# A ninth 2 MB slot for the expert weights, loaded ahead of the expert stage

## Chip, cores and metric

One core of one Trainium2 chip runs the whole program. The metric is device time in microseconds (us), the median of several runs. Engines are named as the profile names them: PE (TensorE matmul), PEld (its weight load), DVE (VectorE), ACT (ScalarE), POOL (GpSimd), SP (SyncE, which here only issues DMAs).

## What is computed

The reference runs two blocks on 256 tokens of width 1024, all in float32.

The first block has two layers of a mixer (attention, a spatial gate, a Fourier mix) and a squared-ReLU MLP, over the tokens and over 256 context tokens.

The second block projects the tokens (`w_in_2`), runs a gated linear recurrence and a chunked linear attention, sums both through `w_out_2`, and normalises. Then comes the mixture of experts:

```python
logits = xt @ w_router + b_router
top_val, top_idx = lax.top_k(logits, TOP_K)          # 4 of 32 experts for each token
...
hdn = xb @ w_up[e] + b_up[e]                         # 1024 -> 2048
gate_h = jnp.minimum(hdn[:, :D_FF_2], SWIGLU_LIMIT)
up_h = jnp.clip(hdn[:, D_FF_2:], -SWIGLU_LIMIT, SWIGLU_LIMIT)
act = (up_h + 1.0) * gate_h * jax.nn.sigmoid(SWIGLU_ALPHA * gate_h)
y = act @ w_down[e] + b_down[e]                      # 1024 -> 1024
```

A second layer norm and a gate through `w_ple_gate` end it. The weights of one expert are 8 MB (`w_up`) and 4 MB (`w_down`); all 32 experts are read, whatever the router chooses.

## The kernel before

Every weight matrix is cut on the host into chunks of 2 MB, 128 partitions by 4096 floats (`CW = 4096`). A chunk lies in a slot of SBUF, and PE reads it from there. `ring(s)` (line 159) says where slot s lies: slots 0 to 2 are the tile RG, slots 3 to 6 are the four quarters of the tile BIG, slot 7 is the end of SM1, and slot 8 is another piece of BIG, used once in the first block. Up to the end of the second block's mixer only the three slots of RG turn over, because BIG holds intermediate results. For the experts eight slots are used: 3, 4, 5, 6, the three of RG in the order in which they come free, then 7. `R.turn` (line 1125) is that order, and chunk i of the expert stage lies in slot `R.turn[i % 8]`. Expert e has the chunks 6e to 6e+5: four of `w_up`, then two of `w_down`. After the 192 chunks of the experts come the two of `w_ple_gate`, numbers 192 and 193. They must lie in slots 3 and 4, since other data lies in the rest of BIG by then.

All weight loads are issued by one engine, SP, in one order (from line 2887). It first walks through the list of early chunks, waiting before each one until PE has finished with the chunk that was in its slot. The last two early chunks are those of `w_out_2`. Then it waits for `s_ym` (line 2915), which DVE raises eight times as it finishes the mixer's output; from there on BIG is free. It loads two small constants, then chunks 0 to 3 into BIG. Chunks 4 to 6 wait for the three RG slots; chunk 7 waits until SM1's end is free (`("z", 7)`, `("pw", 7)`), with the small load of `b_up_rows` between the two waits. From chunk 8 on, chunk i waits for `s_used` to reach i - 7. PE raises `s_used` by one when it has finished a chunk, so load i starts when PE is done with chunk i - 8:

```python
                if i >= 8:
                    sp.wait_ge(s_used, i - 7)
                landing(key, source(key))
```

`landing` (line 2887) starts the DMA, which raises `s_landed` of its slot by 16 when it has landed; `expert_chunk` (line 1127) has PE wait for that before the first matmul on the chunk.

In the expert stage PE does for each expert (`expert`, line 1244): a bias matmul, the scatter of the expert before, 8 matmuls of 128x512 on each of the four `w_up` chunks (line 1275; the profile has 16 records for them), the transposes and the gather for the next expert (lines 1162, 1138, 1297), and 8 matmuls on each of the two `w_down` chunks (line 1312). Expert 1 has more than 64 tokens in this input and takes a wider path (lines 1183 to 1239). DVE and ACT do the activation (lines 2632, 1921, 1929). POOL does nothing in this stage. ACT issued three DMAs (lines 1803 to 1805) earlier; POOL issues none.

Of the kernel before, what the change touches and what calls it, by code (L numbers as in the profile page):

```python
# [12 lines left out]
NEXP = 32  # L13
CW = 4096
# [78 lines left out]
class Ring:  # L93


    def __init__(self):
        self.order, self.slot, self.nth, self.count, self.end, self.now, self.before = [], {}, {}, [0] * 9, {}, {}, {}

    def get(self, key, slot):
        if key not in self.slot:  # L100
# [17 lines left out]
def build(nc, A, out):  # L118
    (T1, W1), (T2, W2) = smalls()
    ctx = ExitStack()  # L120
    with ctx:
        def sb(name, w, p=128):
            return ctx.enter_context(nc.sbuf_tensor(name, [p, w], F32))

        def sem(name):
            return ctx.enter_context(nc.semaphore("s_" + name))
# [4 lines left out]
        CAT_ = sb("CAT", 4096)  # L131
        BIG = sb("BIG", 16384)
        RG = sb("RG", 3 * CW)
        STAT = sb("STAT", 512 * 3)
        MISC = sb("MISC", 1100)
        HOLD = sb("HOLD", 1024)
# [19 lines left out]
        def s2(n, *dims):  # L156
            o, w = T2[n]
            return view(SM1, o, *(dims or (w,)))

        def ring(s):  # L160
            if s < 3:
                return RG[:, s * CW:(s + 1) * CW]
            if s < 7:
                return BIG[:, (s - 3) * CW:(s - 2) * CW]
            if s == 8:
                return BIG[:, 7680:7680 + CW]
            return SM1[:, W2 - CW:W2]

        def own(t, s):
# [3 lines left out]
        s_full = [sem(f"full{i}") for i in range(8)]  # L173
        s_free = [sem(f"free{i}") for i in range(8)]

        s_landed = [sem(f"landed{i}") for i in range(9)]
        s_used = sem("used")
        s_cc, s_sm, s_sm2, s_sm3, s_out = (sem(n) for n in ("cc", "sm", "sm2", "sm3", "out"))

# [66 lines left out]
        F, R = Fills(range(8)), Ring()  # L246
# [36 lines left out]
        WS2 = [view(SM1, o + 512 * i, 4, 128) for i in range(2)]  # L283
        WS4 = [view(STAT, 256 + 768 * i, 4, 128) for i in range(2)]
        AS1, AS2, AS4 = (view(CAT_, 1024 * i, 4, 256) for i in range(3))
# [48 lines left out]
        def stat(s, slot):  # L334
            return STAT[:, 768 * s + 256 * slot:768 * s + 256 * slot + 256]

# [48 lines left out]
        c4b = SV[:, 400:408].rearrange("p (a e) -> p a e", a=2)  # L385
        GTT = STAT[:, 1024:1280]
        IOTA, IOTA2, TRI, ONE1 = HOLD[:, 256:384], HOLD[:, 384:512], HOLD[:, 768:896], onet[:, 0:128]
# [17 lines left out]
        SELG2 = SM1[:, 768:1024].rearrange("p (a s) -> p a s", a=2)  # L405
        SCT = STAT[:, 1280:1536]
        G1_, S1_ = (view(STAT, 512 * i, 2, 256) for i in range(2))
        U1_ = view(HOLD, 0, 2, 512)[:, :, 0:256]
# [31 lines left out]
        def _(pe):  # L440
# [681 lines left out]
            hints = {}  # L1122
            over = pe.alloc_register("pe_over")
            ended = list(F.at)
            R.turn = [3, 4, 5, 6] + sorted(range(3), key=lambda s: ended.index(R.end[R.now[s]])) + [7]

            def expert_chunk(ex, c):
                i = 6 * ex + c
                s, nth = R.get(("expert", ex, c), R.turn[i % 8])
                pe.wait_ge(s_landed[s], 16 * nth)  # L1130
                return ring(s).rearrange("p (k n) -> p k n", k=4)

# [267 lines left out]
                m = pe.matmul(banks[b][:, 0:256], ones, XS[:, k, 0:256], start=k == 0, stop=k == 7)  # L1400
            m.then_inc(s_zfull[b], 1)
            for c in range(2):
                s, nth = R.get(("w_ple_gate", c), R.turn[(6 * NEXP + c) % 8])
                assert s in (3, 4)
                pe.wait_ge(s_landed[s], 16 * nth)
                w = ring(s).rearrange("p (k n) -> p k n", k=8)
                for n in range(4):
                    b = end_take(("e", 4 * c + n))
                    for k in range(8):
                        if c + n == 0:  # L1410
                            pe.wait_ge(s_zg, k + 2)
                        pe.matmul(banks[b][:, 0:257], w[:, k, 128 * n:128 * n + 128], ZG[:, k, :], start=k == 0, stop=False)  # L1412
                    pe.matmul(banks[b][:, 256:257], ID2, s2("b_ple")[:, 4 * c + n:4 * c + n + 1],
                              start=False, stop=True).then_inc(s_zfull[b], 1)
                    if c == 0 and n == 1:
                        b = end_take(("ms",))
                        pe.wait_ge(s_zsum, 7)
                        pe.matmul(banks[b][:, 0:256], ones, SIDE[:, 0, :], start=True, stop=True).then_inc(s_zfull[b], 1)
# [585 lines left out]
        def _(dve):  # L2004
# [354 lines left out]
            post("ff", 0, X)  # L2359
            D.up(dve.memset(STAT[:, 256:257], 1.0))  # L2360
            one = D.n
# [523 lines left out]
        @block.sync  # L2885
        def _(sp):
            def landing(key, src):
                sp.dma_start(ring(R.slot[key]), src).then_inc(s_landed[R.slot[key]], 16)

            def full(key):  # L2890
                b, n, m = F.at[key]
                sp.wait_ge(s_full[b], m)

            def source(key):
                if key[0] == "expert":
                    return A["w_up"][key[1], key[2]] if key[2] < 4 else A["w_down"][key[1], key[2] - 4]
                if len(key) == 2:
                    return A[key[0]][key[1]]
                if key[0].startswith("w_ff"):
                    return A[f"{key[0]}_{key[1]}"][key[2]]  # L2900
                return A[f"{key[0]}{key[1]}"][key[-1]]

            first = T1["ropec"][0]
            sp.dma_start(SM1[:, 0:first], A["sm1"][:, 0:first]).then_inc(s_cc, 16)
            sp.dma_start(own(XS, C), A["xs"][:, C]).then_inc(s_in[C], 16)
            early = [k for k in R.order if k in R.end]
            for i, key in enumerate(early):
                if R.before[key]:
                    full(R.end[R.before[key]])
                landing(key, source(key))  # L2910
                if key == ("w_in", 0, C, 0):
                    sp.dma_start(own(XS, X), A["xs"][:, X]).then_inc(s_in[X], 16)
                if key == ("w_in", 0, C, 1):
                    sp.dma_start(SM1[:, first:W1], A["sm1"][:, first:W1]).then_inc(s_sm, 16)
            sp.wait_ge(s_ym, 8)
            sp.dma_start(HOLD[:, 256:512], A["iota"]).then_inc(s_sm3, 16)
            sp.dma_start(HOLD[:, 768:896], A["tri"]).then_inc(s_sm3, 16)
            for i in range(6 * NEXP + 2):
                key = ("expert", i // 6, i % 6) if i < 6 * NEXP else ("w_ple_gate", i - 6 * NEXP)
                if 4 <= i < 7:  # L2920
                    full(R.end[R.now[R.turn[i]]])
                if i == 7:
                    full(("z", 7))
                    sp.dma_start(BUPR, A["b_up_rows"]).then_inc(s_sm3, 16)
                    full(("pw", 7))
                if i >= 8:
                    sp.wait_ge(s_used, i - 7)
                landing(key, source(key))
            for k0, k1 in (0, 4), (4, 7), (7, 8):
                sp.wait_ge(s_fin, k1)  # L2930
                sp.dma_start(out[:, k0:k1, :], ZO[:, k0:k1, :]).then_inc(s_out, 16)
            sp.wait_ge(s_out, 48)
# [137 lines left out]
```

## Time and profile before

| what | value |
|---|---|
| time, median of 3 runs | 2335.0 us (2332.87 to 2336.21) |
| the profiled execution's own time | 2330.96 us |
| its span, first to last instruction | 2329.2 us |
| granted TensorE clock, mean | 0.996 |
| PE busy | 2224.1 us (95% of the span) |
| DVE, ACT, POOL busy | 771.6, 463.3, 154.1 us |
| read from HBM | 598.20 MB |

The profile is of one execution. Times within it count from the first instruction of the span. The share of DMA is the mean busy share of the core's 16 DMA engines. An idle time stands with what ended it: "<-DMA RG<-in_w_up" says that the engine went on when a load of `w_up` into RG had landed. The chain of waits is followed back from the last instruction, at each step to what released it. In the chain a DMA piece runs from its issue to its landing, so it holds the time in the queue too.

### The profile page before, as it was taken

What the parts mean: (1) busy time and instruction counts of PE and PEld (TensorE: products, weight loads), DVE (VectorE), ACT (ScalarE), POOL (GpSimd) and SP (SyncE); (2) the same over time, 40 slices, a digit from 0 to 9 for tenths busy, and PEclk for the clock granted to TensorE, in tenths of its full rate; (3) what the DMA queues carried; (4) which work ended last, traced back from release to release, by engine and by line L of the source; (5) the groups of instructions that cost most, each with busy time, mean ns of one, the idle gap of its engine ahead of it and who ended that gap; (6) DMA issues with size and microseconds to landing.
All of it is one profiled execution on the core that took longest, in us unless ns stands there. A gap on an engine that the chain in (4) does not pass through costs nothing.

```text
span 2329.2 us, 27569 instructions
## 1 busy us (share of the span) xinstructions
PE 2224.1 (95%) x11292; PEld 1450.0 (62%) x11292; DVE 771.6 (33%) x1789; ACT 463.3 (20%) x1056; POOL 154.1 (7%) x162
## 2 busy tenths in 40 slices
PE   6999999999999999999999999999999899999998
PEld 4777888888887688887688843334333333333335
DVE  2245554578525420004665321112111111111114
ACT  3255411100024532002543210000000000000003
POOL 1000111144301000000000000000000000000000
PEclk9999999999999999999999999999999999999999
DMA  9722212134215444434433768999999999999993
GB/s 387 272 107 109 109 73 109 73 117 173 109 73 193 178 177 165 156 145 175 144 109 143 292 272 343 427 427 427 427 428 427 427 428 428 425 429 428 427 428 141
DMA packets 44264, 601.16 MB, mean 258 GB/s; under 512 B 4705, under 2 KB 7521, under 8 KB 7905
## 3 DMA queue, kind: packets, MB, share of 16 engines
q1 hardware_dynamic: 43696, 595.40, 63.0%
q10 hardware_dynamic: 432, 3.87, 0.4%
q8 instruction: 95, 1.56, 0.3%
q14 instruction: 41, 0.33, 0.0%
HBM read 598.20 MB, written 1.05 MB: 257 GB/s over the span
## 4 chain that ended last, share of the span: by engine, by line
PE 78%; DMA 18%; DVE 2%; ACT 1%; issue 0%; POOL 0%; SPq 0%; POOLq 0%; PEldq 0%; DVEq 0%; ACTq 0%
PE PS L1275 11%; DMA RG<-in_w_up 9%; PE PS L961 8%; DMA BIG<-in_w_up 8%; PE PS L706 7%; PE PS L1312 6%; PE PS L741 6%; PE PS L690 5%; PE PS L793 5%; PE PS L654 3%; PE PS L539 3%; PE PS L779 2%; PE PS L1138 2%; PE PS L1171 2%; PE PS L478 1%; PE PS L1412 1%
## 5 line engine op out<-in xcount | busy, mean ns | idle before, releaser
L2632 DVE TENSOR_SCALAR STAT<-PS 128x256 f32<-128x256 f32 x64 | 27.2, 424 | 709.1 <-PE PS L1275 688.6
L1275 PE MATMUL PS<-BIG,XS 128*64 128x512 f32 x1024 | 230.2, 599 | 23.6 <-DMA BIG<-in_w_up 23.6
L1275 PE MATMUL PS<-RG,XS 128*64 128x512 f32 x768 | 172.6, 597 | 20.2 <-DMA RG<-in_w_up 20.2
L1275 PEld LDWEIGHTS PS<-BIG,XS 128*64 128x64 f32 x1024 | 70.4, 137 | 173.1 <-issue 125.9
L961 PE MATMUL PS<-XS,RG 128*128 128x256 f32 x768 | 173.2, 384 | 5.0 <-DVE XS L2075 4.1
L1461 ACT ACTIVATE BIG<-PS 128x256 f32<-128x256 f32 (+2 forms) x197 | 82.2, 432 | 442.1 <-PE PS L706 138.9
L961 PEld LDWEIGHTS PS<-XS,RG 128*128 128x128 f32 x768 | 146.6, 193 | 26.8 <-issue 6.9
L1921 ACT ACTIVATE STAT<-STAT 128x256 f32<-128x256 f32 x64 | 26.6, 416 | 592.8 <-DVE STAT L2632 592.8
L2041 DVE TENSOR_SCALAR HOLD<-PS 128x256 f32<-128x256 f32 x27 | 11.4, 423 | 380.0 <-PE PS L514 277.9
L1275 PEld LDWEIGHTS PS<-RG,XS 128*64 128x64 f32 x768 | 52.1, 136 | 131.7 <-issue 92.2
L690 PE MATMUL PS<-HN,RG 128*128 128x256 f32 x576 | 125.1, 379 | 1.0 <-ACT HN L1510 1.0
L690 PEld LDWEIGHTS PS<-HN,RG 128*128 128x128 f32 x576 | 109.3, 190 | 16.5 <-issue 1.7
L1312 PE MATMUL PS<-BIG,CAT 128*64 128x512 f32 x512 | 115.1, 598 | 0.8 <-DVE CAT L2658 0.8
L793 PE MATMUL PS<-BIG,RG 128*128 128x256 f32 x512 | 110.7, 379 | 0.0
L793 PEld LDWEIGHTS PS<-BIG,RG 128*128 128x128 f32 x512 | 97.3, 190 | 13.2
L2793 POOL TENSOR_TENSOR HN<-HN 128x256 f32<-128x256 f32 x84 | 63.2, 752 | 629.8 <-ACT HN L1489 206.4
L1312 PE MATMUL PS<-RG,CAT 128*64 128x512 f32 x384 | 86.5, 597 | 0.0
L1312 PEld LDWEIGHTS PS<-BIG,CAT 128*64 128x64 f32 x512 | 34.3, 136 | 69.8 <-issue 60.0
L706 PE MATMUL PS<-HN,RG 128*128 128x256 f32 x336 | 77.3, 379 | 0.0
L539 PE MATMUL PS<-HN,RG 128*128 128x256 f32 x320 | 73.0, 382 | 0.0
L654 PE MATMUL PS<-CAT,RG 128*128 128x256 f32 x320 | 71.5, 381 | 0.0
L706 PEld LDWEIGHTS PS<-HN,RG 128*128 128x128 f32 x336 | 63.8, 190 | 8.7
(400 smaller groups left out, 3251.2 us busy)
## 6 DMA issues: line engine op xcount, KB each, us to landing
BIG<-in_w_up SPq DMA_DIRECT2D x64, 2048.0 KB, 34.1
RG<-in_w_up SPq DMA_DIRECT2D x48, 2048.0 KB, 33.8
BIG<-in_w_down SPq DMA_DIRECT2D x32, 2048.0 KB, 35.4
RG<-in_w_ff SPq DMA_DIRECT2D x31, 2048.0 KB, 7.8
RG<-in_w_ada SPq DMA_DIRECT2D x24, 2048.0 KB, 8.7
RG<-in_w_down SPq DMA_DIRECT2D x24, 2048.0 KB, 35.4
RG<-in_w_in SPq DMA_DIRECT2D x23, 2048.0 KB, 7.9
SM<-in_w_up SPq DMA_DIRECT2D x16, 2048.0 KB, 35.2
```

The source lines that it names most:

```text
L539: m = pe.matmul(banks[b][:, 0:256], w[:, k, c0:c0 + 128], N[:, k, :], start=k == 0, stop=k == 7)
L654: m = pe.matmul(banks[b][:, 0:256], w[:, k, 128 * (n % 4):128 * (n % 4) + 128], own(CAT, s)[:, k, :], start=i == 0, stop=i == 7)
L690: m = pe.matmul(banks[b][:, 0:256], w[:, k, 128 * n:128 * n + 128], own(HN, s)[:, k, :], start=k == 0, stop=k == 7)
L706: m = pe.matmul(banks[b][:, 0:256], w[:, k, :], a[:, k, :], start=not first and k == 0, stop=k == 3, skip_group_check=True)
L741: return pe.matmul(banks[b[j]][:, 256 * half:256 * half + 256], w, a, start=first and half == 0, stop=last, skip_group_check=True)
L779: m = pe.matmul(banks[b[s, o]][:, 0:256], w[:, k, 128 * o:128 * o + 128], own(FFH, s)[:, 16 * h + k, :], start=h + k == 0, stop=h * 16 + k ...
L793: m = pe.matmul(banks[b][:, 0:256], w[:, k, :], own(FFH, s)[:, k, :], start=k == 0, stop=k == 31)
L961: m = pe.matmul(banks[b][:, 0:256], w[:, k, 128 * n:128 * n + 128], src[:, k, 0:256], start=k == 0, stop=k == 7)
L1275: i = pe.matmul(banks[b][64 * h:64 * h + 64, :], XG[:, 4 * (c % 2) + kk, 64 * r:64 * r + 64], w[:, kk, 512 * h:512 * h + 512], start=False ...
L1312: m = pe.matmul(banks[b][64 * h:64 * h + 64, :], AVT[:, i:i + 64], w[:, kk, 512 * h:512 * h + 512], start=c + kk == 0, stop=c == 1 and kk ...
L1461: i = act.activation(dst, banks[b][rows, part], fn)
L2793: S.up(pool.tensor_tensor(H[:, i, :], H[:, i, :], H[:, k, :], ALU.add))
```

## The change

The bookkeeping `Ring` has counters for ten slots. A new tile EXT of 4096 floats (16 KB per partition, 2 MB in all) is allocated behind RG and becomes slot 9. There is one more landing semaphore. The program reserves 1,024 bytes per partition for the descriptors of DMAs that POOL would issue, in place of the default of 16,384.

The expert stage uses nine slots in the order 9, 5, 6, 3, 4, the three of RG, 7. SP issues chunk 0 into slot 9 behind the last early chunk, ahead of its wait for `s_ym`. Chunks 1 to 4 follow the small constants, chunks 5 to 7 wait for RG, chunk 8 for SM1's end, and from chunk 9 on load i waits until PE is done with chunk i - 9. Chunks 192 and 193 fall on slots 3 and 4 as before. The amount of data is the same.

```diff
+        EXT = sb("EXT", CW)
...
+            if s == 9:
+                return EXT[:, :]
...
-        s_landed = [sem(f"landed{i}") for i in range(9)]
+        s_landed = [sem(f"landed{i}") for i in range(10)]
...
-            R.turn = [3, 4, 5, 6] + sorted(range(3), key=lambda s: ended.index(R.end[R.now[s]])) + [7]
+            R.turn = [9, 5, 6, 3, 4] + sorted(range(3), key=lambda s: ended.index(R.end[R.now[s]])) + [7]
...
-                s, nth = R.get(("expert", ex, c), R.turn[i % 8])
+                s, nth = R.get(("expert", ex, c), R.turn[i % 9])
...
+            landing(("expert", 0, 0), source(("expert", 0, 0)))
             sp.wait_ge(s_ym, 8)
             sp.dma_start(HOLD[:, 256:512], A["iota"]).then_inc(s_sm3, 16)
             sp.dma_start(HOLD[:, 768:896], A["tri"]).then_inc(s_sm3, 16)
-            for i in range(6 * NEXP + 2):
+            for i in range(1, 6 * NEXP + 2):
                 key = ("expert", i // 6, i % 6) if i < 6 * NEXP else ("w_ple_gate", i - 6 * NEXP)
-                if 4 <= i < 7:
+                if 5 <= i < 8:
                     full(R.end[R.now[R.turn[i]]])
-                if i == 7:
+                if i == 8:
                     full(("z", 7))
                     sp.dma_start(BUPR, A["b_up_rows"]).then_inc(s_sm3, 16)
                     full(("pw", 7))
-                if i >= 8:
-                    sp.wait_ge(s_used, i - 7)
+                if i >= 9:
+                    sp.wait_ge(s_used, i - 8)
                 landing(key, source(key))
...
-    nc = bacc.Bacc("TRN2", target_bir_lowering=False, num_devices=1)
+    nc = bacc.Bacc("TRN2", target_bir_lowering=False, num_devices=1, dynamic_dma_scratch_size=1024)
```

## Rows read from the trace of the kernel before

**Rows 1.** The page's head: busy time of each engine over the span.

```profile
PE 2224.1 (95%) x11292; PEld 1450.0 (62%) x11292; DVE 771.6 (33%) x1789; ACT 463.3 (20%) x1056; POOL 154.1 (7%) x162
```

**Rows 2.** Busy time by stretches: start:end, length, engines, PEclk, DMA share, GB/s.

```profile
1275.00:1297.00 22.00, 22.00 (x110) 19.52 (x109) 12.96 (x26) 5.29 (x11) 0.00 (x0) 1.00 0.26 96
1340.00:1356.00 16.00, 15.27 (x103) 10.40 (x103) 4.55 (x23) 4.93 (x10) 0.00 (x0) 0.93 0.02 7
1356.00:1431.00 75.00, 71.38 (x526) 30.01 (x528) 14.61 (x40) 6.35 (x11) 0.00 (x0) 1.00 0.86 337
1431.00:1645.00 214.00, 214.00 (x1084) 83.93 (x1082) 40.80 (x112) 16.23 (x32) 0.00 (x0) 1.00 1.00 425
1645.00:2290.00 645.00, 589.49 (x2911) 221.02 (x2908) 112.56 (x308) 44.02 (x87) 0.00 (x0) 1.00 1.00 426
```

**Rows 3.** PE's waits from 1645 to 2290 us: us in total, times, longest.

```profile
PE PS L1275 <- DMA BIG<-in_w_up: 23.6, 19, 2.8
PE PS L1275 <- DMA RG<-in_w_up: 20.2, 18, 1.2
PE PS L1275 <- DMA SM<-in_w_up: 8.6, 7, 1.2
```

**Rows 4.** The chain of waits in the expert stage: start, length, what.

```profile
1352.34 3.58 PE PS L1275 x16
...
1585.86 13.88 PE PS L1275 x64
...
1612.34 13.88 PE PS L1275 x64
...
1645.88 35.20 DMA RG<-in_w_up
...
1763.31 35.24 DMA RG<-in_w_up
...
1822.05 36.80 DMA BIG<-in_w_up
...
2236.30 35.26 DMA RG<-in_w_up
```

**Rows 5.** PE's timeline, first waits: start, length, [idle before <- what ended it].

```profile
1638.76 7.09 PE L1275 MATMUL PS<-RG,XS 128*64 128x512 f32 x32
...
1676.24 3.65 PE L1275 MATMUL PS<-RG,XS 128*64 128x512 f32 x16 [1.07 <-DMA RG<-in_w_up]
1681.13 3.65 PE L1275 MATMUL PS<-RG,XS 128*64 128x512 f32 x16 [1.24 <-DMA RG<-in_w_up]
```

**Rows 6.** PE's timeline at the end of the last expert.

```profile
2271.60 3.65 PE L1275 MATMUL PS<-RG,XS 128*64 128x512 f32 x16 [1.24 <-DMA RG<-in_w_up]
...
2281.38 3.65 PE L1312 MATMUL PS<-SM,CAT 128*64 128x512 f32 x16
...
2293.43 3.71 PE L1412 MATMUL PS<-BIG 128*128 128x257 f32 x16 [1.21 <-ACT BIG L1974]
```

**Rows 7.** SP's DMA issues from 1255 us on: start, from first to last issue.

```profile
1257.25 17.94 SPq L2888 DMA_DIRECT2D RG<-in_w_out  x2
1297.41 0.33 SPq L2916 DMA_DIRECT2D HOLD<-in_iota  x1
...
1298.26 2.08 SPq L2888 DMA_DIRECT2D BIG<-in_w_up  x4
...
1333.46 0.33 SPq L2888 DMA_DIRECT2D SM<-in_w_up  x1
1355.97 5.84 SPq L2888 DMA_DIRECT2D BIG<-in_w_up  x2
```

**Rows 8.** DMA queues (packets, MB, share); one source's loads, KB each, us to landing.

```profile
q1 hardware_dynamic: 43696, 595.40, 63.0%
q10 hardware_dynamic: 432, 3.87, 0.4%
...
RG<-in_w_out SPq DMA_DIRECT2D x8, 2048.0 KB, 7.9
```

More of the change, by code:

```diff
@@ L96, in __init__ @@
     def __init__(self):
-        self.order, self.slot, self.nth, self.count, self.end, self.now, self.before = [], {}, {}, [0] * 9, {}, {}, {}
+        self.order, self.slot, self.nth, self.count, self.end, self.now, self.before = [], {}, {}, [0] * 10, {}, {}, {}
     def get(self, key, slot):
@@ L1402, in _ @@
             for c in range(2):
-                s, nth = R.get(("w_ple_gate", c), R.turn[(6 * NEXP + c) % 8])
+                s, nth = R.get(("w_ple_gate", c), R.turn[(6 * NEXP + c) % 9])
                 assert s in (3, 4)
```

## The prediction

> **What bounds the kernel now.** I read the page's head first. PE is busy for 95% of the span [rows 1], which suggests that only PE work counts. The stretches say otherwise for the last 650 us [rows 2]. From 1431 us on the DMA engines have a share of 1.00 and bring 425 or 426 GB/s, up to 2290 us. In the first part of that, up to 1645 us, PE is busy without a gap. In the second it is idle for 645.00 - 589.49 = 55.5 us. PE's own waits name the cause of 52.4 us of it (23.6 + 20.2 + 8.6): loads of w_up that had not landed [rows 3]. There are 44 such waits, two per expert.
>
> The chain of waits gives the two speeds [rows 4]. Before 1645 us it runs through PE alone, and one expert takes 1612.34 - 1585.86 = 26.48 us. After 1645 us each piece of about 35 us is a DMA, from issue to landing. Two experts then take 1822.05 - 1763.31 = 58.74 us, which is 12 chunks, so one chunk takes 4.895 us of the DMA queue and one expert 29.37 us. DMA is slower than PE by 2.89 us per expert. PE starts with eight chunks in hand, lives on them until 1645.9 us, and from there runs at the speed of the queue. The last wait of this kind ends at 2271.60 us [rows 6]. What follows is fixed work behind the last loads.
>
> So the end is set by a full queue: the moment from which it never runs empty, plus the chunks that it still has to bring, at 4.895 us each. The change must be priced by what it does to this sum. PE's busy share says nothing on it.
>
> **Where the queue is not full.** Chunks 0 to 3 are issued at 1298.26 us, and the issue for chunk 7 is at 1333.46 us [rows 7]. From 1340 to 1356 us the DMA share is 0.02 [rows 2]: all eight slots are full, and PE has not finished a chunk. At 1355.97 us it has, and chunk 8 is issued. From 1356 to 1431 us the share is 0.86: a load starts whenever PE ends a chunk, and the queue sometimes runs dry. From 1431 us on it never does. Ahead of all this, from 1275 to 1297 us, the share is 0.26 and the rate 96 GB/s: that is the second chunk of w_out_2, issued at 1257.25 + 17.94 - 0.33 = 1274.86 us, and then nothing. SP stands at its wait for s_ym there.
>
> **The change, part by part.**
>
> 1. Chunk 0 moves ahead of the wait for s_ym. SP issues it at about 1275.2 us, just behind the second chunk of w_out_2. That chunk lands 7.9 us after its issue by the median [rows 8], at 1282.8 us, and chunk 0 one transfer later, at about 1287.7 us. The queue was empty then and stays empty until 1297.41 us, so the 4.9 us of transfer cost nothing. The issue takes 0.33 us of SP, which waits there for some 22 us. It holds back nothing: s_ym releases SP at 1297.4 us as before.
>
> 2. The loads behind the wait keep their times and shift by one in number. At 1298.26 us four loads into BIG go out, now chunks 1 to 4. The three RG slots get chunks 5 to 7 as they come free, as they got 4 to 6. Then b_up_rows goes out with as many bytes ahead of it as before, and SM1's end gets chunk 8 at 1333.46 us. When PE ends its first chunk at 1355.97 us [rows 7], chunk 9 is issued where chunk 8 was. PE is not held up by loads before 1645.9 us, so it ends every chunk at the old time up to there, and every issue up to there stands where it stood. The queue sees the same transfers at the same times up to 1431 us and is full afterwards. Chunk i + 1 therefore lands when chunk i landed before. From the last chunk's view: **-4.9 us**.
>
> 3. Bounds of this term. The transfer of one chunk in a full queue is 4.895 us [rows 4]. The most that one chunk can be worth is its time from an empty queue, 7.9 us [rows 8], if its start-up were saved as well. The least is 0, if the lead is lost somewhere before the queue is full. I take the full-queue value, since chunks 9 and on stand in a full queue.
>
> 4. One more DMA wait is postponed. With a chunk more in hand, PE reaches the queue's speed later. Without its waits PE would come to the chunk that it waited for at 1676.24 us [rows 5] at 1638.76 + 7.09 + 26.48 = 1672.3 us. That chunk now lands at 1676.2 - 4.9 = 1671.3 us, in time. The next one lands at 1681.1 - 4.9 = 1676.2 us, and PE comes for it at about 1675.9 us. So the first wait moves from 1646 to about 1676 us, and the waits of rows 3 fall by 4.9, from 52.4 to about 47.5 us. This is the same 4.9 us seen from PE, not a second gain.
>
> 5. The order 9, 5, 6, 3, 4 in place of 3, 4, 5, 6, one more semaphore, and the counters: 0. Chunks 1 to 4 wait for the same event and all of BIG comes free with it; landing semaphores cost PE one wait per chunk as before. Should the order matter after all, there is room: PE starts on chunk 0 at 1352.34 us [rows 4], and chunk 4 should land some 22 us after its issue at 1298.26 us (7.9 + 3 x 4.9).
>
> 6. The smaller reserve for descriptors: 0. It serves DMAs that POOL issues; the queues are those of SP and ACT [rows 8], and POOL issues none. EXT moves other tiles to other addresses, which no row prices; I take 0.
>
> 7. The end. The last expert's third and fourth w_up chunks, its w_down chunks and those of w_ple_gate all land 4.9 us earlier. PE runs from 2271.60 us by its own work except for the last w_down chunk, whose matmuls start at 2281.38, just two transfers after 2271.60, so that one moves with the queue as well. The gate's matmuls at 2293.43 us wait for ACT [rows 6], which moves with PE.
>
> Sum: -4.9 us. Against the profiled execution's own time, 2330.96 us, that gives 2326.1 us, and a span of 2324.3. The median of the runs is 4.0 us above the profiled execution, so I predict **2330.1 us**.
>
> **A rule weighed against a row.** For HBM to SBUF transfers the Trainium skill, "SBUF — State Buffer", section "Summary: rules for kernel authors", says to reckon with about 358 GB/s. By that figure a chunk of 2,097,152 bytes would take 5.86 us, an estimate from that page, and the sum would be -5.9 us. The trace disagrees: 425 to 426 GB/s stand over the whole full stretch [rows 2], and 4.895 us per chunk in the chain. The measured value is used.
>
> **The rivals.**
>
> A. No gain: 2335.0 us. The lead would be lost before 1431 us, for instance because PE's releases come later, or because the profile's empty stretch is not empty in other runs. For it: the stretch from 1356 to 1431 us is bound by releases and not by bytes. Against it: an empty stretch that keeps its place costs the new kernel what it cost the old one. Chance 0.06.
>
> B. The bubbles mean too few buffers, and with one more the queue is better used. Each of the 44 waits would go, and the time would be 2335.0 - 52.4 = 2282.6 us. Against it: the DMA share is 1.00 during these very waits [rows 2, 3], so there is no idle time of the queue to fill. Chance 0.01. The Trainium skill, "Perfetto Trace Analysis", section "Identifying the Most-Contended Engine", reads repeating bubbles on the engine that should be busy as a possible sign of too little SBUF for the next tile; by that rule this rival is the natural reading, and the trace speaks against it.
>
> C. More than one chunk, by some 3 to 6 us: the start-up of a load in the release-bound stretch is saved as well, -7.9 us or somewhat more, 2327 us or less. For it: the share of 0.86 there. Against it: issues and depth of the queue are the same there. Chance 0.04.
>
> D. Slower. One DMA piece of the chain took 36.80 us in place of 35.24 [rows 4], so now and then a chunk needs 1.56 us more. Of the pieces between 1645.88 and 2236.30 us two of eleven are of this kind. Up to eight loads are in flight in the full stretch now; there will be nine. If the longer queue brought such a hiccup once in nine chunks, from about 1676 us on, then (2271.6 - 1676) / 4.9 = 121 chunks would have 13.5 of them, 21 us, and the sum would be 21 - 4.9 = +16 us: 2351 us. It decides from the fourth extra hiccup on (4.9 / 1.56 = 3.1). Nothing in the rows ties the hiccups to depth: between 1645 and 2236 us the depth is the same everywhere, and they are rare. Chance 0.03.
>
> **How the numbers follow.** The forecast case has 0.86. A measurement of this kernel can tell about 0.2% from no change, which is 4.7 us; the forecast of 4.9 us lies just beyond that bound. The three runs of before spread over 3.3 us, so a median may be off by one or two. Of the 0.86 I give 0.47 to faster by over 0.2% and 0.39 to within 0.2%. A adds 0.06 to the same, B and C 0.05 to faster, D 0.03 to slower. Sum: 0.52, 0.45, 0.03. The range: the lower end is the upper bound of the term, 2335.0 - 7.9 = 2327.1, rounded to 2327; the upper end is the forecast with the spread of a median, nearly up to A, 2334. That leaves out D, B and most of A, and the tails of the measurement.
>
> **What would show each step.** Part 1: one issue of a w_up load at about 1275.2 us into EXT, ahead of the iota load at 1297.4. Part 2: the issue times of rows 7 unchanged, and a DMA share near 0.02 again from 1340 to 1356 us. Part 3: the last wait for a w_up load ends at 2266.7 us in place of 2271.6. Part 4: the first DMA wait of PE is at about 1676 us, waits of about 47.5 us in total, and the chain's DMA pieces grow from 35.2 to 40.1 us, one transfer more in the queue. Part 7: the stretch from the last wait to the end is unchanged at 57.6 us. The prediction is wrong if issues before 1431 us move, if the time per chunk differs from 4.895 us, or if pieces with 1.56 us more become frequent.

## The result, and the profile after

The change makes the kernel slightly faster. Over 22 runs of each the median went from 2332.05 to 2328.01 us, 4.0 us less. The ratio is 0.9982, with a 95% interval of 0.9975 to 0.9988, which is 2.8 to 5.8 us less. The forecast was 4.9 us less and 2330.1 us. Note that the median of the kernel before is 2332.05 us over 22 runs and was 2335.0 us over the three that the prediction had, so the absolute time was forecast from a start 3 us too high.

The profiled execution took 2324.32 us, with a span of 2322.4 us, which is 6.8 us less than before. The page's head:

```profile
PE 2223.3 (96%) x11292; PEld 1451.4 (62%) x11292; DVE 772.2 (33%) x1789; ACT 463.0 (20%) x1056; POOL 154.1 (7%) x162
```

PE is as busy as in [rows 1], to within a microsecond. The stretches, with the columns of [rows 2]:

```profile
1275.00:1297.00 22.00, 22.00 (x110) 19.55 (x109) 11.48 (x25) 4.97 (x10) 0.00 (x0) 1.00 0.44 184
1340.00:1356.00 16.00, 15.26 (x104) 9.91 (x104) 3.03 (x14) 3.49 (x8) 0.00 (x0) 1.00 0.09 16
1356.00:1431.00 75.00, 71.38 (x526) 29.17 (x526) 14.59 (x40) 6.31 (x11) 0.00 (x0) 1.00 0.87 338
1431.00:1645.00 214.00, 214.00 (x1084) 84.01 (x1082) 41.75 (x115) 16.64 (x33) 0.00 (x0) 1.00 1.01 427
1645.00:2285.00 640.00, 588.71 (x2911) 222.49 (x2908) 112.57 (x307) 43.80 (x87) 0.00 (x0) 1.00 1.00 425
```

The first stretch has risen from 96 to 184 GB/s: that is chunk 0. The empty stretch is still empty but for its last 2 us (16 GB/s; the first load that a release starts falls into this window, since this execution runs early, as the next rows show). The release-bound stretch is unchanged (0.87, 338 GB/s), and the full one is as full as before. SP's issues, as in [rows 7]:

```profile
1273.31 0.43 SPq L2891 DMA_DIRECT2D EXT<-in_w_up  x1
1295.49 0.33 SPq L2920 DMA_DIRECT2D HOLD<-in_iota  x1
...
1331.53 0.33 SPq L2891 DMA_DIRECT2D SM<-in_w_up  x1
1354.04 0.33 SPq L2891 DMA_DIRECT2D EXT<-in_w_up  x1
```

All of this execution runs 1.92 us ahead of the one before: the iota load, which marks the moment at which s_ym releases SP, is issued at 1295.49 us in place of 1297.41. Up to 1273 us both kernels issue the same loads in the same order, and another execution of the changed kernel (control, below) had the iota load at 1297.67 us, so I take the 1.92 us for scatter between executions. Relative to the iota load the issues stand where they stood: SM1's end at +36.04 us (+36.05 before), the first release at +58.55 (+58.56 before). PE's timeline, first waits and last waits, as in [rows 5, 6]:

```profile
1674.34 3.65 PE L1278 MATMUL PS<-RG,XS 128*64 128x512 f32 x16 [0.45 <-DMA RG<-in_w_up]
...
2259.94 3.65 PE L1278 MATMUL PS<-SM,XS 128*64 128x512 f32 x16 [1.08 <-DMA SM<-in_w_up]
2264.83 3.65 PE L1278 MATMUL PS<-EXT,XS 128*64 128x512 f32 x16 [1.24 <-DMA EXT<-in_w_up]
```

From the iota load to the end of the last wait it took 2264.83 - 1295.49 = 969.34 us. Before it was 2271.60 - 1297.41 = 974.19. That is 4.85 us less: one chunk of the queue. The rest of the 6.8 us in the spans is the scatter ahead of it. PE's waits from 1600 to 2290 us, as in [rows 3]:

```profile
PE PS L1278 <- DMA BIG<-in_w_up: 18.8, 15, 2.8
PE PS L1278 <- DMA RG<-in_w_up: 14.5, 13, 1.3
PE PS L1278 <- DMA EXT<-in_w_up: 8.4, 7, 1.2
PE PS L1278 <- DMA SM<-in_w_up: 6.4, 6, 1.1
```

They sum to 48.1 us in place of 52.4. The chain of waits, as in [rows 4]:

```profile
1640.58 33.72 DMA RG<-in_w_up
...
1694.35 38.68 DMA EXT<-in_w_up
...
1753.08 38.69 DMA BIG<-in_w_up
...
1811.83 40.23 DMA RG<-in_w_up
```

Two experts take 1811.83 - 1753.08 = 58.75 us (58.74 before). Two of the chain's eleven DMA pieces are some 1.5 us longer (40.23 and 40.21 us), also as before.

### The profile page after: what moved, and what is told of

It is laid out like the page before. It is cut to its first block, busy times and chain, and to the rows that moved or that the text cites. A ratio compares the mean times of both kernels' runs of the same rounds, so it can differ in the third digit from the quotient of the medians.

```text
span 2322.4 us, 27569 instructions
## 1 busy us (share of the span) xinstructions
PE 2223.3 (96%) x11292; PEld 1451.4 (62%) x11292; DVE 772.2 (33%) x1789; ACT 463.0 (20%) x1056; POOL 154.1 (7%) x162
## 4 chain that ended last, share of the span: by engine, by line
PE 76%; DMA 20%; DVE 2%; ACT 1%; issue 0%; POOL 0%; SPq 0%; POOLq 0%; PEldq 0%; DVEq 0%; ACTq 0%
PE PS L1278 9%; PE PS L964 8%; PE PS L709 7%; DMA EXT<-in_w_up 7%; DMA RG<-in_w_up 7%; PE PS L1315 6%; PE PS L744 6%; PE PS L693 5%; DMA BIG<-in_w_up 5%; PE PS L796 5%; PE PS L657 3%; PE PS L542 3%; PE PS L782 2%; DMA RG<-in_w_ada 2%; PE PS L1141 2%; PE PS L1174 2%
## 5 line engine op out<-in xcount | busy, mean ns | idle before, releaser
L1278 PE MATMUL PS<-BIG,XS 128*64 128x512 f32 x848 | 191.1, 600 | 18.8 <-DMA BIG<-in_w_up 18.8
L1278 PE MATMUL PS<-RG,XS 128*64 128x512 f32 x672 | 150.4, 596 | 14.5 <-DMA RG<-in_w_up 14.5
L1278 PEld LDWEIGHTS PS<-BIG,XS 128*64 128x64 f32 x848 | 58.9, 137 | 143.2 <-issue 104.2
L693 PEld LDWEIGHTS PS<-HN,RG 128*128 128x128 f32 x576 | 109.4, 190 | 16.3 <-issue 1.7
L1278 PEld LDWEIGHTS PS<-RG,XS 128*64 128x64 f32 x672 | 46.0, 137 | 111.8 <-issue 82.4
L1278 PE MATMUL PS<-EXT,XS 128*64 128x512 f32 x352 | 80.2, 598 | 8.4 <-DMA EXT<-in_w_up 8.4
L1315 PEld LDWEIGHTS PS<-BIG,CAT 128*64 128x64 f32 x528 | 35.2, 136 | 68.8 <-issue 62.2
L1315 PE MATMUL PS<-RG,CAT 128*64 128x512 f32 x336 | 76.5, 597 | 0.0
## 6 DMA issues: line engine op xcount, KB each, us to landing
BIG<-in_w_up SPq DMA_DIRECT2D x53, 2048.0 KB, 38.7
RG<-in_w_up SPq DMA_DIRECT2D x42, 2048.0 KB, 38.7
BIG<-in_w_down SPq DMA_DIRECT2D x33, 2048.0 KB, 40.1
EXT<-in_w_up SPq DMA_DIRECT2D x22, 2048.0 KB, 38.7
RG<-in_w_down SPq DMA_DIRECT2D x21, 2048.0 KB, 40.1
```

What stands on the lines that cost most here:

```text
L693: m = pe.matmul(banks[b][:, 0:256], w[:, k, 128 * n:128 * n + 128], own(HN, s)[:, k, :], start=k == 0, stop=k == 7)
L1278: i = pe.matmul(banks[b][64 * h:64 * h + 64, :], XG[:, 4 * (c % 2) + kk, 64 * r:64 * r + 64], w[:, kk, 512 * h:512 * h + 512], start=False ...
L1315: m = pe.matmul(banks[b][64 * h:64 * h + 64, :], AVT[:, i:i + 64], w[:, kk, 512 * h:512 * h + 512], start=c + kk == 0, stop=c == 1 and kk ...
```

## The experiments

All were compared with runs of the kernel before on the same chip. One number is read from each trace besides the time: the stretch from the start of PE's first matmul on chunk 12 (the first of expert 2) to the end of its last wait for a w_up load (chunk 189). I chose it after the first runs had shown that the time ahead of it scatters; the expectations use two older yardsticks, from the iota load or from PE's first matmul on chunk 0 to that last wait, and their numbers are given too. It is 2271.60 - 1426.90 = 844.70 us before and 2264.83 - 1425.01 = 839.82 us after, 4.88 us less. I call it the full stretch. The rows of the two kernels at chunk 12, from PE's timeline (before, then after):

```profile
1426.90 10.52 PE L1275 MATMUL PS<-RG,XS 128*64 128x512 f32 x48
```

```profile
1425.01 7.09 PE L1278 MATMUL PS<-BIG,XS 128*64 128x512 f32 x32
```

Two theories stood against each other over the runs. Theory 1 is that of the prediction in its simplest form: what counts is the number of bytes that are held when PE ends its first chunk. Theory 2 came up in the course: what counts is what is held when the queue runs dry for the last time.

**slot_only: the slot without the early load.**

```diff
-            landing(("expert", 0, 0), source(("expert", 0, 0)))
             sp.wait_ge(s_ym, 8)
...
-            for i in range(1, 6 * NEXP + 2):
+            for i in range(0, 6 * NEXP + 2):
```

> Nine slots as in the change, but chunk 0 is loaded behind the wait for s_ym with the others. I measure from SP's issue of the iota load (the moment at which s_ym releases it) to the end of PE's last wait for a w_up load: 974.19 us before (2271.60 - 1297.41), 969.34 after the change (2264.83 - 1295.49). Theory 1 (only the number of bytes held when PE ends its first chunk counts): the empty stretch of the queue before that moment was 16 us, so one more chunk of 4.9 us still fits into it, and the stretch stays at 969.3, 0 to 0.5 more since b_up_rows lands at about +44.7 us in place of +39.8 and is wanted at about +45. Rival (the early start pays): 974.2, the time of before.

Measured: ratio 0.9981 (0.9971 to 0.9992), the same gain as with the early load. PE's timeline:

```profile
1428.40 7.09 PE L1278 MATMUL PS<-BIG,XS 128*64 128x512 f32 x32
...
2268.27 3.65 PE L1278 MATMUL PS<-EXT,XS 128*64 128x512 f32 x16 [1.25 <-DMA EXT<-in_w_up]
```

The full stretch is 839.87 us, as after the change. But from the iota load (1295.61 us) to the last wait it was 972.66 us, neither the 969.3 of theory 1 nor the 974.2 of its rival. PE's first matmul on chunk 0 had come 57.48 us after the iota load in place of 54.86. I first took that for a cost of the later b_up_rows; the rows below say otherwise, since PE does not wait there but runs at half its clock. So the kernel was run again.

**slot_only_again.** The same kernel.

> The same kernel as slot_only. There PE's first matmul on chunk 0 came 57.48 us after the iota load in place of 54.86, with the granted clock at 0.50 for 8 us just before (4 us of 0.73 after the change). If that belongs to the order of the loads, it is 57.5 again; if it is chance of where the clock fell, it is 54.9 to 56.5 and the whole stretch 969.3 to 970.5.

Measured, in one execution: 59.15 us from the iota load to the first matmul, outside both cases of the expectation, and 2332.17 us in all. From the iota load to the last wait it was 975.82 us, so by that yardstick the two executions cannot tell theory 1 from its rival. That the gain is there without the early load rests on the ratio over ten runs, which excludes the rival's 1.000, and on the full stretch, 2271.21 - 1431.41 = 839.80 us here. The stretches of the two and of the changed kernel just ahead of the experts; the column before the last two is the granted clock (first the changed kernel, then slot_only, then slot_only_again):

```profile
1338.00:1342.00 4.00, 4.00 (x40) 3.85 (x38) 3.23 (x19) 2.66 (x6) 0.00 (x0) 0.73 0.08 33
1342.00:1346.00 4.00, 3.26 (x23) 2.77 (x15) 1.58 (x7) 0.98 (x2) 0.00 (x0) 1.00 0.02 4
```

```profile
1338.00:1342.00 4.00, 4.00 (x21) 4.00 (x20) 3.06 (x17) 2.57 (x6) 0.00 (x0) 0.50 1.08 455
1342.00:1346.00 4.00, 3.67 (x26) 2.89 (x26) 1.31 (x6) 0.58 (x2) 0.00 (x0) 0.50 0.20 86
1346.00:1350.00 4.00, 4.00 (x18) 3.46 (x17) 0.60 (x2) 1.19 (x2) 0.00 (x0) 0.89 0.02 4
```

```profile
1338.00:1342.00 4.00, 4.00 (x21) 4.00 (x21) 3.06 (x17) 2.43 (x6) 0.00 (x0) 0.50 1.02 430
1342.00:1346.00 4.00, 3.70 (x26) 2.90 (x27) 1.31 (x6) 0.72 (x2) 0.00 (x0) 0.50 0.23 94
1346.00:1350.00 4.00, 4.00 (x12) 3.17 (x11) 0.60 (x2) 0.60 (x1) 0.00 (x0) 0.54 0.00 0
```

With the 4 us ahead of these rows, where the granted clock was already 0.84, 0.83 and 0.76, the clock stands at its lower level for about 3 us in the changed kernel, 10 in slot_only and 14 in slot_only_again, and the first matmul comes 2.6 and 4.3 us late. My expectation left that open between the order of the loads and chance. Two kernels further down, more_later and two_halves, have the early load and still start 57.5 us after the iota load, so the late start also occurs with it. Whether the order makes it more frequent is not settled by two executions; the ratio over ten runs shows no cost.

**early_only: the early load without a ninth slot.** EXT takes the place of SM1's end.

```diff
+            R.turn = [9, 3, 4, 5, 6] + sorted(range(3), key=lambda s: ended.index(R.end[R.now[s]]))
...
+                s, nth = R.get(("expert", ex, c), R.turn[i % 8])
...
+                if i >= 8:
+                    sp.wait_ge(s_used, i - 7)
```

> Chunk 0 is loaded early into EXT, but SM1's end is no slot any more, so there are eight as before. Theory 1: 974.2 us from the iota issue to the last wait, as before, and the time of before, ratio 1.000; first DMA wait of PE about 350 us after the iota load, as before (1645.9 - 1297.4). Rival (the early start pays): 969.3 us, ratio 0.998.

```profile
1426.13 3.65 PE L1278 MATMUL PS<-BIG,XS 128*64 128x512 f32 x16
...
2270.77 3.65 PE L1278 MATMUL PS<-RG,XS 128*64 128x512 f32 x16 [1.24 <-DMA RG<-in_w_up]
```

Measured: ratio 1.0001 (0.9989 to 1.0013). The full stretch is 844.64 us, that of before. From the iota load it was 974.95 us (974.2 expected, 969.3 by the rival). The early load alone brings nothing; the rival falls.

**seven_slots: one slot fewer than before.** Neither EXT nor SM1's end is used for the experts, and there is no early load, as in the kernel before.

```diff
+            free = sorted(range(3), key=lambda s: ended.index(R.end[R.now[s]]))
+            R.turn = [5, 6, free[0], 3, 4] + free[1:]
...
+                if i >= 7:
+                    sp.wait_ge(s_used, i - 6)
```

> Seven slots: four quarters of BIG, three of RG; neither EXT nor SM1's end. Theory 1: one chunk fewer than before in hand, 974.2 + 4.9 = 979.1 us, about +4.9 us against before (ratio 1.002), and the chain's DMA pieces shrink to about 30.3 us. PE's first DMA wait comes about 50 us earlier than before. Rival (slots beyond the first few bring less than a transfer each, or the queue's depth matters): anything clearly off 979.1.

```profile
1428.05 7.09 PE L1279 MATMUL PS<-RG,XS 128*64 128x512 f32 x32
...
2277.49 3.65 PE L1279 MATMUL PS<-BIG,XS 128*64 128x512 f32 x16 [1.24 <-DMA BIG<-in_w_up]
```

Measured: ratio 1.002 (1.001 to 1.003). The full stretch is 849.44 us, 4.74 more than before. From the iota load it was 982.09 us, 3.0 above what I expected: 1.6 us of that lie ahead of the first matmul on chunk 0 and 1.5 us between it and chunk 12, both outside the full stretch and both where the granted clock fell (see the last section). Seven, eight and nine slots give 849.44, 844.70 and 839.82 us, steps of 4.74 and 4.88. The chain's DMA pieces were some 30.5 us long (35.2 with eight slots, 38.7 with nine).

**more: three eighths of a slot in addition, for chunk 9.** Chunk 9's first 1536 columns go into space that is free by then, 1024 floats in SM1 and 512 in a new tile.

```diff
+                if i == 9:
+                    sp.dma_start(ring(R.slot[key])[:, 1536:4096], source(key)[:, 1536:4096]).then_inc(s_landed[R.slot[key]], 16)
+                    continue
                 landing(key, source(key))
+                if i == 8:
+                    sp.dma_start(PART1, source(("expert", 1, 3))[:, 0:1024]).then_inc(s_cc, 16)
+                    sp.dma_start(PART2[:, :], source(("expert", 1, 3))[:, 1024:1536]).then_inc(s_cc, 16)
```

> The change plus 3/8 of a slot: the first 1536 of the 4096 floats of chunk 9 are loaded behind chunk 8 into space that is free by then (1024 floats in SM1, 512 in a new tile), and the load at the first release brings only the rest. Theory 1: -4.9 x 3/8 = -1.8 us against the change: 967.5 us from the iota issue to the last wait, and -6.7 us against before (ratio 0.9971). Rival (the ninth slot used up what the empty stretch gives, or small loads cost as much as they bring): 969.3 or more.

```profile
1425.18 7.09 PE L1294 MATMUL PS<-BIG,XS 128*64 128x512 f32 x32
...
2264.81 3.65 PE L1294 MATMUL PS<-EXT,XS 128*64 128x512 f32 x16 [1.24 <-DMA EXT<-in_w_up]
```

Measured: ratio 0.9987 (0.9976 to 0.9998), and the full stretch is 839.63 us, 0.2 less than after the change. From the iota load it was 969.13 us. The 1.8 us of theory 1 did not come. Either theory 1 is wrong, or the small loads cost what they bring; this run alone does not tell the two apart, cut_before and more_later below do. Theory 2 has a reason: in the stretch from 1356 to 1431 us the queue still runs dry several times, for the last time at the issue of the load for chunk 20 with eight slots, of chunk 21 with nine. The kernel before there, by SP's issue and by stretches of 2 us:

```profile
1430.60 3.76 SPq L2888 DMA_DIRECT2D RG<-in_w_up  x2
```

```profile
1427.00:1429.00 2.00, 2.00 (x10) 0.67 (x12) 0.00 (x0) 0.00 (x0) 0.00 (x0) 1.00 1.04 434
1429.00:1431.00 2.00, 2.00 (x12) 0.72 (x10) 0.00 (x0) 0.00 (x0) 0.00 (x0) 1.00 0.06 25
1431.00:1433.00 2.00, 2.00 (x12) 0.61 (x10) 0.00 (x0) 0.00 (x0) 0.00 (x0) 1.00 0.81 180
1433.00:1435.00 2.00, 2.00 (x12) 0.68 (x10) 0.86 (x3) 0.42 (x1) 0.00 (x0) 1.00 0.94 401
```

"Dry" has to be taken with care: by the trace's landings the load ahead landed 0.7 us after this issue, but the DMA engines had next to nothing left to do (share 0.06), and chunk 20 landed 8.35 us after chunk 19. The loads behind it land 4.9 us apart. This issue comes when PE ends chunk 12, whatever was saved before. A whole slot more survives this, because it shifts the number of the chunk that is issued there. Saved bytes don't. In the eleven profiles with whole loads there, the load issued when PE ended chunk 12 landed 12.5 to 12.8 us after PE's start on chunk 12, whether it was that of chunk 19 (seven slots), 20 (eight) or 21 (nine); more and cut_before are among them, with 12.6 us.

**cut_before and cut_after: bytes taken away on either side of the last dry moment.** In one kernel 7/8 of the load of chunk 9 are left out, in the other 7/8 of that of chunk 31. Both compute with old data in these places, so they measure time only.

```diff
+                if i == 9:
+                    sp.dma_start(ring(R.slot[key])[:, 0:512], source(key)[:, 0:512]).then_inc(s_landed[R.slot[key]], 16)
+                    continue
```

> Leaves out 7/8 of the load of chunk 9 (columns 512 to 4095 of that w_up chunk), the first load that is issued when PE ends a chunk. I measure from PE's first matmul on chunk 0 to the end of its last wait for a w_up load: 919.32 us before, 914.49 after the change. Theory 1 (bytes are bytes, wherever in the stage they are saved): 914.5 - 4.3 = 910.2. Theory 2 (the queue runs dry for the last time about 78 us after PE's first matmul, and bytes saved ahead of that are lost; only what shifts the number of the chunk issued at that moment counts): 914.5, unchanged.

> Leaves out 7/8 of the load of chunk 31 in place of chunk 9: that load is issued after the queue's last dry moment. Both theories: 914.5 - 4.3 = 910.2 us, and about -4.3 us against the change in the whole time. Only a time that does not move would speak against both.

```profile
1427.91 7.09 PE L1278 MATMUL PS<-BIG,XS 128*64 128x512 f32 x32
...
2267.80 3.65 PE L1278 MATMUL PS<-EXT,XS 128*64 128x512 f32 x16 [1.24 <-DMA EXT<-in_w_up]
```

```profile
1425.67 7.09 PE L1278 MATMUL PS<-BIG,XS 128*64 128x512 f32 x32
...
2261.24 3.65 PE L1278 MATMUL PS<-EXT,XS 128*64 128x512 f32 x16 [1.24 <-DMA EXT<-in_w_up]
```

The diff is that of cut_before; cut_after has 31 in place of 9. Measured, in one execution of each (2327.18 and 2320.74 us in all): 839.89 us with the bytes missing before the dry moment, 835.57 us with them missing after it. The difference is 4.3 us, the time of 7/8 of a chunk. From the first matmul, as the expectations have it, it was 915.26 and 910.78 us. The saving ahead of the dry moment is lost entirely, without any small load in play: theory 1 falls here, and theory 2 stands.

**halves: loads 9 to 35 in two halves, released by halves.**

```diff
+                            if not broad and h == kk == 1:
+                                i.then_inc(s_ym, 1)
...
+                if 9 <= i < 36:
+                    lo = 0
+                    for part, a, b in (s_ym, lo, 2048), (s_used, 2048, 4096):
+                        sp.wait_ge(part, i - 8 + 8 * (part is s_ym))
+                        sp.dma_start(ring(R.slot[key])[:, a:b], source(key)[:, a:b]).then_inc(s_landed[R.slot[key]], 16)
+                    continue
```

> The change, with loads 9 to 35 issued in two halves of 1 MB, each as soon as PE has finished with that half of the slot. Theory 2: the last refill from empty starts when PE is halfway through its 13th chunk, 1.8 us earlier, so the stream is full 1.8 to 3 us earlier: 912 to 912.7 us from the first matmul to the last wait, ratio about 0.9972 to before (the change has 0.9982). Theory 1 has only the first release 1.8 us earlier and expects the same -1.8; what would speak against theory 2 is 914.5 or more. Rival: smaller loads and twice the issues cost as much as they bring, 914.5 or more.

```profile
1430.08 7.09 PE L1286 MATMUL PS<-BIG,XS 128*64 128x512 f32 x32
...
2270.09 3.65 PE L1286 MATMUL PS<-EXT,XS 128*64 128x512 f32 x16 [1.24 <-DMA EXT<-in_w_up]
```

Measured: ratio 0.9986 (0.9977 to 0.9995), the full stretch 840.01 us, and 915.07 us from the first matmul. The expected gain did not come, and 915.07 is beyond the 914.5 that the expectation named as speaking against theory 2 or for loads in halves that cost what they bring. The landings speak for the second: a lead was won and spent. The whole of chunk 22 had landed 91.0 us after the first matmul, 92.3 after the change, and chunk 36 at 160.7 against 160.9. Over these 14 chunks a pair of halves took about 0.08 us more than a whole. Counted from PE's start on chunk 12 the lead is 1.7 us at chunk 22, as theory 2 has it, and 0.5 us at chunk 36. At chunk 189 it is 0.2 us behind, though the loads after chunk 35 are whole; this last 0.7 us is not explained.

**more_later: the same three eighths, for chunk 33.** The diff is against the kernel more.

```diff
-                if i == 9:
+                if i == 33:
...
-                    sp.dma_start(PART1, source(("expert", 1, 3))[:, 0:1024]).then_inc(s_cc, 16)
+                    sp.dma_start(PART1, source(("expert", 5, 3))[:, 0:1024]).then_inc(s_cc, 16)
```

> As the kernel more, the first 1536 of 4096 floats of one chunk are loaded behind chunk 8 into space that is free by then, but of chunk 33 in place of chunk 9. The issue of chunk 33's load comes after the queue's last dry moment, that of chunk 9's before it. From PE's first matmul on chunk 0 to the end of its last wait for a w_up load: 914.49 us after the change, 914.27 with more. Theory 2 (bytes saved ahead of the last dry moment are lost, bytes held across it are gained): 914.5 - 4.9 x 3/8 = 912.7. Theory 1 (bytes held at PE's first release count) expects the same of both kernels; 914.3 here would speak for small loads that cost what they bring.

```profile
1430.02 7.09 PE L1294 MATMUL PS<-BIG,XS 128*64 128x512 f32 x32
...
2267.89 3.65 PE L1294 MATMUL PS<-EXT,XS 128*64 128x512 f32 x16 [1.25 <-DMA EXT<-in_w_up]
```

Measured, in one execution (2327.25 us in all): the full stretch is 837.87 us, 1.95 less than after the change, where the same parts for chunk 9 gave 0.2. From the first matmul it was 914.07 us, since the part ahead of chunk 12 was 1.5 us slower than in the change's profile; that accounts for the 1.4 us by which the 912.7 of the expectation was missed. Held across the dry moment, the bytes count, and small loads don't eat them.

**two_halves: only loads 21 and 22 in halves.** The diff is against the kernel halves.

```diff
-                if 9 <= i < 36:
+                if i in (21, 22):
```

> As the kernel halves, but only the loads 21 and 22, the ones with which the queue is refilled for the last time, are issued in two halves. In halves the second half of chunk 22 had landed 91.0 us after PE's first matmul, against 92.3 after the change, and by chunk 36 the lead was gone (160.7 against 160.9): 14 chunks in halves took 0.08 us more each. Theory: without the other halves the lead of 1.3 us stays, 913.2 us to the last wait (911.5 at best, 1.8 us if the whole half-chunk of PE's time is gained). Rival (halves save nothing): 914.5.

```profile
1431.33 7.09 PE L1286 MATMUL PS<-BIG,XS 128*64 128x512 f32 x32
...
2270.48 3.65 PE L1286 MATMUL PS<-EXT,XS 128*64 128x512 f32 x16 [1.25 <-DMA EXT<-in_w_up]
```

Measured, in one execution (2331.54 us in all, above the median of the changed kernel): 839.15 us, 0.67 less than after the change, half of the expected 1.3 us. From the first matmul it was 915.98 us, 1.5 more than after the change, since chunk 12 began 2.2 us later after it. That the halves gain rests on the full stretch of this one execution.

**both, and control.** The last two edits together, and the changed kernel once more beside it.

> more_later and two_halves together. If both add, 914.5 - 1.8 - 1.3 = 911.4 us from the first matmul to the last wait, 7.9 us less than before: ratio to before 0.9966, against 0.9982 for the change. Where the granted clock falls just ahead of the experts can move single runs by some 2 to 4 us.

> The changed kernel once more, beside the others on the same chip: ratio to before 0.998, 914.5 us from the first matmul to the last wait. From the iota load to the first matmul 54.9 us, or 1.5 to 4.5 us more if the clock falls in another place; this tells how much of the scatter comes from there.

```profile
1425.86 7.09 PE L1301 MATMUL PS<-BIG,XS 128*64 128x512 f32 x32
...
2263.19 3.65 PE L1301 MATMUL PS<-EXT,XS 128*64 128x512 f32 x16 [1.24 <-DMA EXT<-in_w_up]
```

```profile
1427.94 7.09 PE L1278 MATMUL PS<-BIG,XS 128*64 128x512 f32 x32
...
2267.72 3.65 PE L1278 MATMUL PS<-EXT,XS 128*64 128x512 f32 x16 [1.24 <-DMA EXT<-in_w_up]
```

Measured: both (7 runs) has a ratio of 0.9970 (0.9959 to 0.9981), median 2325.03 us; control (12 runs) has 0.9984 (0.9976 to 0.9993), median 2328.86 us; before had 2332.0 us beside them. From the first matmul it was 912.41 us (911.4 expected) and 915.20 us (914.5 expected). The full stretches are 837.33 and 839.78 us. So both is 2.45 us ahead of the change and 7.37 ahead of before in the trace. Of the versions that load all weights it is the fastest found. The two intervals overlap, so that it beats the change rests on the trace more than on the times.

## Why the prediction was right

The mechanism and its size were right: one chunk of the full queue, 4.895 us forecast, 4.85 us measured from the iota load and 4.88 us in the full stretch. The measured change of the medians is 4.0 us, with an interval of 2.8 to 5.8 us that holds the forecast. The prediction gave 0.52 to a gain of over 0.2% and 0.45 to less. At 0.18% the ratio lies just on the less favoured side, and its interval, 0.12 to 0.25%, does not decide.

Part 1 held: chunk 0 was issued at 1273.31 us, 22.2 us ahead of the iota load, and the stretch in which it is carried had room. What I did not say is that the early issue is no part of the gain. slot_only has the gain without it, and early_only has it without the gain. The prediction's own part 2 would have allowed the conclusion: the empty stretch of 16 us has room for one more load of 4.9 us.

Part 2 held to 0.1 us: the issues keep their distance from the iota load, and the number of the chunk shifts by one. Its reason was sound, since it argued from every issue up to the last dry moment and not from bytes held at the first release. The simpler form in which I carried it into the experiments was wrong: more gave the first sign, and cut_before showed it.

Part 3: the full-queue value was the right one. The upper bound of 7.9 us, with the start-up of a load saved, was not needed: the refill from empty is still there, with another chunk in it.

Part 4: the first wait of PE was expected at about 1676 us and ended at 1674.34 us, in an execution that ran 1.9 us early; with that it is right to 0.3 us. The waits fell to 48.1 us, 47.5 expected. The chain's DMA pieces were expected at 40.1 us and are 38.7. That reading was wrong, without effect on the time: with nine slots the chain passes through the load issued at the end of an expert's first chunk, and not of its second. PE takes two w_up chunks there without a wait, 3.5 us each, so the issue moves forward by 3.5 us and not by 4.9. The last wait ended at 2264.83 us and not at 2266.7; the difference of 1.9 us is again the early run.

Parts 5 and 6: at no cost that any run shows. early_only has EXT, the smaller reserve and another order, and has the time of before (1.0001). Part 7: from the last wait to the end it was 57.6 us, as forecast. Five of the fourteen profiles, control among them, took 59.2.

The rivals. A, no gain, is out: the interval excludes it. B, the bubbles as a lack of buffers, is out: 41 waits are left of 44, and seven, eight and nine slots change the time by one transfer each, not the rate. The rate in the full stretch stayed at 425 to 427 GB/s. The Trainium skill, "Perfetto Trace Analysis", has the sentence on bubbles that the prediction cites in its section "Optimization Strategy". C, more than one chunk, did not happen, and more and cut_before show why: whatever is saved ahead of the last dry moment is gone. D, slower by hiccups with nine loads in flight, is out: there are two longer pieces in the chain's eleven, as before. The landings say it more fully: from chunk 37 to 189 three loads came 6.0 to 6.5 us after the one ahead in place of 4.9, with seven, eight and nine slots alike.

The rule of 358 GB/s that was weighed in the prediction is qualified by another page of the Trainium skill, "HBM Reference", section "Specifications (TRN2)": a core that streams alone reaches about 425 GB/s. With 425 to 427 GB/s in the full stretch the trace agrees.

The number fell near the lower end of the range, 2327 us, and the start is the reason: 2335.0 us was 3 us above the median of 22 runs. That worked against the forecast of 2330.1 us, not for it. With the gain as forecast and the later median, 2327.2 us would have come out, 0.8 us from the 2328.01 measured.

## What to carry to other kernels

Where a prefetch ring feeds an engine that is faster than the queue, as here, the end is set by the last moment at which the queue runs dry. One more slot was worth one transfer, once, from seven to eight and from eight to nine, and did not change the rate. Bytes saved or loaded early ahead of that moment were worth nothing; the same bytes held across it counted in full. Look for that moment first, by the DMA share in short stretches, and use spare memory for a load that is issued behind it.

To see an effect of 0.2%, measure within the trace between two events that lie on the mechanism. Here five profiles of kernels that have the same bytes to bring behind the dry moment gave that stretch as 839.78 to 839.89 us, while whole times of one kernel scattered over 12 us.

## What the runs showed of the hardware that I had not expected

Part of the scatter between executions has a source that can be read. Just ahead of the experts PE works in small pieces with waits between them, and the granted clock falls from 1.00 to 0.50, its lower level of 1.2 GHz, for a time that differs from run to run. From the iota load to the first matmul on chunk 0 it took 54.9 us in eight of the fourteen profiles, with the clock low for about 3 us; 56.5 us in two (7 us low), 57.5 in three (10 us) and 59.2 in one (14 us). The two executions of slot_only had 57.5 and 59.2; seven_slots and the kernel before, without the early load too, had 56.5 and 54.9. In four profiles, seven_slots and more_later among them, the clock fell again within expert 1, after a wait of 2.3 us for DVE (0.63 from 1406 to 1410 us in seven_slots), and PE's next eight matmuls took 3.2 to 3.6 us in place of 2.0. These losses count, since they delay the releases that the queue waits for.

In the full stretch the same fall costs nothing. In nine of the fourteen profiles the clock fell for some 3 us between 2057 and 2077 us, behind PE's longest waits for a load (0.57 from 2060 to 2064 us after the change), and in the others it did not. Four of the five full stretches of 839.78 to 839.89 us had this fall and cut_before had not. At the end it counts again: in control the last w_down matmuls took 8.78 us in place of 7.23, with the granted clock at 0.86 in those 10 us, and the end came 1.6 us later.

A refill of the queue from empty takes longer than a transfer. After the change the loads for chunks 9 and 19 were issued 13.8 and 3.0 us after the last landing and landed 7.6 us after their issue, where a load in the full queue lands 4.9 us after the one ahead. The load for chunk 21, issued 0.6 us before the load ahead landed, took 9.1 us from issue to landing, 8.45 us after the load ahead; the next one landed 4.9 us after it.

The full queue has a late load now and then: after the change those of chunks 61, 103, 147 and 192 landed 6.3 to 6.4 us after the one ahead in place of 4.9, some 207 to 222 us apart. With seven and eight slots they were nearly the same chunks (60, 103, 147, 192). Why is not shown.
